# A ring of sixteen gathered rows beside a ring of four weight units

## What is computed

```python
def peer_ffn(h, w_q, sub_keys, u, v):
    q = (ht @ w_q).reshape(T, PEER_HEADS, 2, PEER_QDIM // 2)
    s = jnp.einsum('thpd,pnd->thpn', q, sub_keys)
    top_s, top_i = lax.top_k(s, PEER_TOPK)
    ...
    best_s, best_j = lax.top_k(cand_s.reshape(T, PEER_HEADS, -1), PEER_TOPK)
    experts = jnp.take_along_axis(cand_i..., best_j, axis=-1)
    gates = jax.nn.softmax(best_s, axis=-1)
    def chunk(args):
        act = jax.nn.gelu(jnp.einsum('cd,ced->ce', xc, u[ec]))
        return jnp.einsum('ce,ced->cd', gc * act, v[ec])
```

## Time and profile before

| | us |
|---|---|
| median of 3 runs | 2664.3 |
| lowest, highest | 2661.26, 2667.13 |
| the profiled execution | 2653.54 |
| its span | 2651.9 |

### The profile page before, as it was taken

The page is one execution under the profiler, slowest core; times in us unless marked ns, Lnnn a source line. Parts: engine busy times, 40 slices in busy tenths (PEclk is TensorE's granted clock), DMA queues, the critical chain, the costliest instruction groups (busy, mean ns, idle before and its releaser), DMA issues.

```text
span 2651.9 us, 23297 instructions
## 1 busy us (share of the span) xinstructions
PE 1790.7 (68%) x7234; PEld 1217.1 (46%) x7234; DVE 1618.2 (61%) x3441; ACT 370.0 (14%) x977; POOL 1212.9 (46%) x1124
## 2 busy tenths in 40 slices
PE   7999689998968056665556666556566765255565
PEld 6887578886847034431145244225443632011112
DVE  3348425402154986688665756886476598667764
ACT  1012401000121021100112211011121110000001
POOL 1001001100000476467764775676467467777774
PEclk9899899998969568886878878877878877667768
DMA  9547348842415489999998898999979988899996
GB/s 322 186 161 232 121 129 326 308 154 98 135 40 191 152 308 338 350 371 328 358 365 352 319 352 332 341 340 350 383 259 342 349 317 318 313 374 397 396 374 250
DMA packets 210157, 757.92 MB, mean 286 GB/s; under 512 B 23036, under 2 KB 26248, under 8 KB 209800
## 3 DMA queue, kind: packets, MB, share of 16 engines
q0 software_dynamic: 161280, 587.27, 60.2%
q1 hardware_dynamic: 48344, 167.35, 18.0%
q10 hardware_dynamic: 432, 2.03, 0.2%
HBM read 755.50 MB, written 1.07 MB: 285 GB/s over the span
## 4 chain that ended last, share of the span: by engine, by line
PE 36%; POOL 21%; DMA 17%; DVE 16%; issue 8%; ACT 2%; POOLq 0%; DVEq 0%; ACTq 0%
PE psL L423 30%; POOL W L414 21%; DMA W<-experts_v,crow 15%; PE psS L423 3%; PE psO L423 2%; DVE W L908 2%; DVE Z L843 1%; DMA W<-experts_u,crow 1%; DVE N L843 1%; DVE bias L1313 1%; DVE Z L849 1%; PE psT L536 1%; DVE bias L1316 1%; DVE Sb L843 1%; ACT W L1432 1%
## 5 line engine op out<-in xcount | busy, mean ns | idle before, releaser
L423 PE MATMUL psL<-W,con 128*128 128x512 f32 x1024 | 666.2, 793 | 502.5 <-DMA W<-experts_v,crow 359.4
L414 POOL DMA_INDIRECT W<-experts_u,crow x512 | 602.7, 1177 | 672.5 <-DVE crow L846 358.8
L908 DVE SCALAR_TENSOR_TENSOR W<-W,Z 128x1024 f32<-128x1024 f32 x512 | 618.8, 1225 | 326.8 <-DMA W<-experts_u,crow 323.7
L414 POOL DMA_INDIRECT W<-experts_v,crow x512 | 559.2, 1092 | 283.2 <-PE psL L423 140.7
L423 PE MATMUL psL<-N,wring 128*128 128x256 f32 (+1 forms) x3568 | 627.4, 339 | 74.8 <-DVE N L846 60.7
L423 PEld LDWEIGHTS psL<-W,con 128*128 128x128 f32 x1024 | 227.2, 242 | 888.0 <-issue 732.7
L423 PEld LDWEIGHTS psL<-N,wring 128*128 128x128 f32 x3568 | 566.0, 201 | 147.3 <-DVE N L846 65.0
L843 DVE SCALAR_TENSOR_TENSOR Z<-W,crow,Z 128x1024 f32<-128x1024 f32 x252 | 323.6, 1284 | 104.7 <-DMA W<-experts_v,crow 100.7
L398 POOL DMA_DIRECT2D aring<-ada x96 | 50.9, 530 | 454.7 <-DVE aring L1038 453.8
L1432 ACT ACTIVATE Z<-psL 128x128 f32<-128x128 f32 (+2 forms) x190 | 60.4, 319 | 627.6 <-PE psL L423 627.6
L536 PE MATMUL psT<-con,Pb 128*128 128x128 f32 x144 | 34.6, 364 | 162.9 <-DVE Pb L846 162.9
(11 more groups left out here) (197 smaller groups left out, 1371.8 us busy)
## 6 DMA issues: line engine op xcount, KB each, us to landing
wring<-weights SPq DMA_DIRECT2D x311, 512.0 KB, 4.8
aring<-ada POOLq DMA_DIRECT2D x96, 512.0 KB, 5.8
W<-experts_u,crow POOLq DMA_INDIRECT x512, 6.3
W<-experts_v,crow POOLq DMA_INDIRECT x512, 6.2
W<-rel_rows SPq DMA_DIRECT2D x1, 1536.0 KB, 9.0
X<-x_dram ACTq DMA_DIRECT2D x1, 1024.0 KB, 6.0
out<-N SPq DMA_DIRECT2D x1, 1024.0 KB, 3.9
W<-rel_rows SPq DMA_DIRECT2D x1, 768.0 KB, 4.9
```

The costliest lines, as they stand in the source:

```text
L414: pool.indirect_dma_start(W[:, slot * D:(slot + 1) * D], None, experts_u if kind == "u" else experts_v, bass.IndirectOffsetOnAxis(ap=idx[: ...
L423: return pe.matmul(o, l, r, start=first, stop=last)
L908: dve.scalar_tensor_tensor(out=row, in0=row, scalar=1.0, in1=h_t[T], op0=ALU.mult, op1=ALU.mult, accum_out=dots[:, col:col + 1]).then_inc( ...
```

## The change

The ring of rows gets 16 slots. The room (eight buffers of 4 KB a partition) comes from two places: `aring` is no longer a tile of its own but lies in slots 8 to 11 of `W`, and the ring of weights keeps four units of eight. A round stays 8 places (ROUND). `FK` is gone with `aring`: the forget term is now, for each head, the queries' row times the head's indicator, kept in `N` (free at that time), times the keys' row that stands in `Z`.

```diff
-WRING = 8
+WRING = 4
 ARING = 4
-GRING = 8
+GRING = 16
+ROUND = 8
...
-NROUND = PER // GRING
+NROUND = PER // ROUND
...
-        aring = sb("aring", [P, ARING, D])
...
-        FK = aring[:].rearrange("p a d -> p (a d)")
+        aring = W[:, 8 * D:(8 + ARING) * D].rearrange("p (a d) -> p a d", a=ARING)
...
             g = UNIT0[name] + j
-            eng.wait_ge(landed[g % WRING], (i + g // WRING + 1) * 16)
+            eng.wait_ge(landed[g % WRING], (i * (8 // WRING) + g // WRING + 1) * 16)
...
-                    for p in range(r * GRING, (r + 1) * GRING):
+                    for p in range(r * ROUND, (r + 1) * ROUND):
...
-                        slot = p % GRING
+                        slot = (t * PER + p) % GRING
...
-                            last = mm(o, lrow[r, 0:P], FK[r, h * S:h * S + w], False, True)
+                            last = mm(o, N[r, h * P:(h + 1) * P], toks(Z, OF, 0, r, w), False, True)
...
-                    m = ts(FK[:, h * S + T * P:h * S + (T + 1) * P], f, C("ind", 1, P, h), None, ALU.mult)
+                    m = ts(N[:, h * P:(h + 1) * P], row, C("ind", 1, P, h), None, ALU.mult)
```

More of the change, by code:

```diff
@@ L891, in rows @@
                 for r in range(stream["done"], min(stream["done"] + n, NROUND)):
-                    for p in range(r * GRING, (r + 1) * GRING):
+                    for p in range(r * ROUND, (r + 1) * ROUND):
                         kind, i = PLACE[p]
                         who, count = FREED[t * PER + p]
-                        slot, col = p % GRING, T * SLOTS + i
+                        slot, col = (t * PER + p) % GRING, T * SLOTS + i
                         row = W[:, slot * D:(slot + 1) * D]
```

## The result

The changed kernel took 2577.4 us (median of 4 runs, 2572.5 to 2581.1) against 2665.1 for the one before; the ratio is 0.968, 95% interval 0.966 to 0.971. The forecast was 2560, with a range from 2480 to 2625. The profiled execution took 2572.5 us, its span 2570.8: 81 us less than the one shown before, where 104 were expected.

The account below looks back on a forecast made before the run. The gather stream, with producer and consumer waiting for each other on a too short ring, was taken as the bound. -146 + 19 + 15 + 8 = -104 from 2653.5, plus 10.8 to the median, gave 2560 us, range 2480 to 2625.

Parts of the forecast that it names:

- The bound: First row to last tile: gather stream limits; POOL waits 309.5 us for slots, DVE 310.1 us for rows, at different moments.
- The ring, -146: Row ring from 8 to 16 slots, first row to last tile: saves 146 us of the 309.5 us slot waits.
- the rule that a stretch gains the smallest of three waits: Each stretch saves at most the least of POOL's slot waits, DVE's row waits and DMA idle time; 57.2 us in one period.
- the first rival: Stock carried over: a ring full after a DVE-bound stretch feeds the DMA-bound one behind; 2480 us, chance 0.10.
- the factor 0.50: Third period's 57.2 us gain over its 114.9 us slot waits, applied to all 309.5 us, giving 154 before a correction.
- (a): Gathers beside DVE: POOL works 87% instead of 78% of the time, so its gathers slow; +19 us.
- (b): Within stretches of the row stream, some waits come in the wrong order to offset; +15 us, ends 0 and 73.
- another wait takes the place: Where DVE stops waiting for rows it may wait for PE and ACT; a third of 104 left, 2629 us, chance 0.10.
- (c): Weights ring from 8 to 4 units: wide stages stay covered, narrow ones may make PE wait; +8 us, between 0 and 127.
- The lower DMA limit: Row stream can sustain only the last tile's 371 GB/s, not 410; 2587 us, chance 0.04.
- Weights: Narrow projections: PE stands for units, DVE behind it, costing more than the rows give; 2699 us, chance 0.05.
- unused depth: Slots are freed in order; if PE's late row holds POOL, the ring is full at 16 as at 8; 2664, chance 0.03.

Follow-up runs that it names:

- a_b3: Changed kernel with four rounds of rows instead of two (three in the first tile) beside the first half of the query projection; 2563.6 us, ratio 0.962.
- a_ps: Changed kernel with the second operand of the last tile's u product read from PSUM instead of SBUF; 2574.0 us, ratio 0.968.
- w4g8: Kernel before with only the four-unit weights ring, eight row slots kept, ada in W and the new forget term; 2660.8 us, ratio 1.001.
- w4g12: Against the kernel before: four-unit weights ring and twelve row slots; 2589.0 us, ratio 0.974.
- w8g12: Against the kernel before: twelve row slots, the eight-unit weights ring kept; 2587.5 us, ratio 0.973.
- w2g18: Against the kernel before: two-unit weights ring and eighteen row slots; 2790.9 us, ratio 1.051.
- a_b3p: a_b3 with GpSimd, at three output projections, waiting for one more finished unit before every second of eight gathers; 2498.7 us, ratio 0.943.
- a_half: Changed kernel with gathers bringing only partitions 0 to 63 after the first sixteen, so half the bytes; 2613.7 us, ratio 0.981.
- b_b3: Kernel before (eight slots, eight units) with the rounds of rows of a_b3; 2663.4 us, ratio 1.005.
- b_again: The kernel before, unchanged, profiled once more; 2659.8 us, ratio 0.999.
- a_hold: Changed kernel with GpSimd's next gather at three output projections waiting until that projection's first four units are done; 2595.0 us, ratio 0.973.

## Why the prediction was right, and where its terms were not

**The bound** was named rightly: the stream between the first row and the last tile, with producer and consumer waiting for each other. All the gain lies there, the last tile kept its length, and the plateau rose (to 363 rather than 370 GB/s).

**The ring, -146.** Too large. POOL's waits for slots fell to 197 to 212 us, not to 165, or by 72 us without the 0.30 ahead of each gather; DVE's waits for rows fell further than forecast, to 114 and not 165, and came back elsewhere. For the third tile the four stretches were to give 57 us; between the same rounds, at the borders of the forecast, they gave 29:

| part of the third tile | forecast | before | after | gave |
|---|---|---|---|---|
| odd projection (end of r0 to end of r6) | 5.5 | 98.7 | 84.2 | 14.5 |
| attention (to the end of r16) | 26.5 | 146.2 | 141.5 | 4.7 |
| output projection, first queries (to r20) | 9.4 | 62.4 | 62.6 | -0.2 |
| search and the rest (to the next tile) | 15.8 | 153.3 | 143.1 | 10.2 |

The step that did not hold is the rule that a stretch gains the smallest of three waits. Two of the three belonged to engines that had something later to wait for. In the part from r16 to r20 the DMA engines idled 9.4 us and DVE waited for rows, and both stood in the shadow of the chain output projection, norm, queries, scores: with rows in stock DVE reaches its end earlier and waits there, 18.4 us at 2038. a_b3 shows this, by getting some of it back with the same ring. In the attention the rounds r7 to r16 themselves became 25 us shorter, near the forecast's 26.5, but 12 came back between r15 and r16, where unit 3 of the output projection is seen done 10 us late, and 7 ahead of r7. The odd projection gained 9 more than the minimum allowed; stock carried over, the first rival's mechanism, would do that, and no run tests it apart. A second, smaller error of size: of 111 slot waits each held the 0.30 us that stands ahead of any gather; I took this off for seven of them. At the factor 0.50 that is 17 us too many.

**(a) GpSimd slower, +19.** Nothing. A gather took 1.150 us on average in the three tiles before and (287.32 + 299.61 + 291.08)/768 = 1.143 after. The scaling by POOL's busy share was the wrong step. A likely reason: the excess arises per row that DVE works on, the rows are the same in number, and a POOL that stands less sends more gathers beside an idle DVE (74 before, 110 now), which are the short ones (0.94 us). That two SBUF operands slow a gather was right: a_ps took one away and the mean fell by 0.07 us.

The Trainium skill, SBUF — State Buffer, "Who interferes with whom", infers that descriptor writing isn't held up. The prediction says that the trace speaks against this; it doesn't. The loads of ada are the plain case: GpSimd issues them too, and L1038 on DVE has two SBUF inputs of 128x1024 like a u row. In the changed kernel, all 96 of them (duration ns min/median/max), and one beside a row of L1038:

```profile
L398 POOL DMA_DIRECT2D W<-ada x96: 527/527/711, 1.4 to 504.0; - x96
...
75.77 1.22 DVE L1038 SCALAR_TENSOR_TENSOR W<-W,crow 128x1024 f32<-128x1024 f32 x1
...
76.50 0.53 POOL L398 DMA_DIRECT2D W<-ada  x1 [0.61 <-DVE W L1038]
```

All the 38 loads that overlap L1038 by over 0.3 us took 0.527 to 0.530 us, and none of the 96 took less. So both halves of the page agree with these traces. That zero came out for (a), as by the Trainium skill, has another reason: the gathers are held up, before and after alike.

**(b) the order of waits, +15.** Right in kind and too small, with the upper bound of 73 near: of 146 us 65 did not come. This is the term into which the shortfall belongs, and the mirror of the rival "another wait takes the place", which priced it at a third of 104. It did happen, in the places where DVE waits for TensorE and ScalarE: these waits grew by 114 us while those for rows fell by 196. How much of it is the rule and how much the late units can't be parted: the waits for outputs of a projection, +48 us, are where the late units show, the trace of before had none of them, and the changed kernel was not run on the chip without them.

**(c) the four-unit ring, +8.** Nothing (w4g8, and w4g12 against w8g12). The pace of 2.56 us came as worked out, and the cover, that each narrow stage waits for rows anyway, held also with a deeper ring. The wide stages kept their cover as computed: the traces show no wait of a row's worth there, and with two units it is gone (w2g18). PE's waits on wring in the changed kernel are 12.1 us in 17 cases, up to 2.5 us, as said.

So the sum was near, -104 against -81, because (a), (c) and a too large gain partly set each other off: 27 us charged that did not arise and 50 credited that did not come. That the forecast came within 23 us is in part luck.

**The rivals.** Carried stock: perhaps in one part, and the time is far off. The lower DMA limit of 371 GB/s gave 2587, nearer than my forecast. It is not shown by that. The odd projections of the changed kernel ran at 384 GB/s over 117 us, above its limit, and a_b3p has 382 in the last tile; a_half's last tile keeps its length at half the bytes, though not at half the engines' time (78% busy instead of 96). The 358 GB/s that the Trainium skill gives as HBM's share of one core (DMA: Bandwidth & Descriptors, "Where 436 GB/s comes from") is passed by the same rows, so it bound nothing in this program on one core. Weights and unused depth: excluded by w4g8 and w4g12.

## What to carry to other kernels

In this kernel the deeper ring paid only as far as its consumer could take the stock. Before building one, list what the consumer waits for right behind each wait that you remove, above all where a serial chain (projection, norm, scores) has its end, and give the stock rounds to go to at those places (a_b3), since the same order is worth nothing with a shallow ring (b_b3). Halving the ring of weights was free, since behind its delays the projections waited for rows anyway; measure such a trade by itself, once with the old depth of the other ring. And where one engine feeds all transfers, look at its own time per transfer before the bandwidth: 1.40 us a gather is 375 GB/s, whatever the memory could do.

## What the hardware showed unexpectedly

- Units of TensorE are seen done late by VectorE, ScalarE and SyncE alike, up to 13 us in the changed kernel, 16 in a_half and 18 in w2g18, mostly until 1 to 3 us after the end of a run of gathers on GpSimd; on some chips or executions in every kernel, in others never, and only in traces that also lack semaphore events. What holds them isn't known. With 8 slots it costs nothing measurable (b_again 2659.8 against 2662.3 us).
- A gather into 64 partitions isn't half a gather: 1.00 us of GpSimd instead of 1.10 in the last tile, 0.22 us a packet instead of 0.155, and a kernel that is some 35 us slower than with all of the bytes.
- Beside an idle VectorE a gather takes 0.93 to 0.96 us and 0.30 us stand between two, as in 19 of the 20 in a row of a_hold. Beside VectorE's work with two SBUF operands it takes up to 1.99 us, with one of the two in PSUM 0.94 (a_ps); a plain load that GpSimd issues keeps its 0.53 us beside such work.
